# A three-mixer transformer and a mixture of experts in one program: two token row groups of the input projection moved into the mixers

## What is computed

```python
for l in range(DEPTH):                    # DEPTH = 2
    h = x @ w_cols                        # 3400 columns, 3432 in the second layer
    o_gla  = _gla_mixer(gq, gk, gv, gg, galr, ...)
    o_rwkv = _rwkv7_mixer(rr, rk, rv, rwlr, ralr, rglr, ...)   # token shift first
    o_nsa  = _nsa_mixer(h_nsa, pos, ...)  # rotary q and keys, compressed blocks, gates
    mix = jnp.concatenate([o_gla, o_rwkv, o_nsa], axis=-1) @ w_out[l]
    x = _layer_norm(DEEPNORM_ALPHA * x + mix, ln1_w[l], ln1_b[l])
    ffn = (jax.nn.silu(x @ ffn_w_gate[l]) * (x @ ffn_w_up[l])) @ ffn_w_down[l]
    x = _layer_norm(DEEPNORM_ALPHA * x + ffn, ln2_w[l], ln2_b[l])
```

## Time and profile before

| | |
|---|---|
| median of 3 runs | 2019.58 us (2018.89 to 2026.96) |
| the profiled execution | 2023.03 us, its span 2021.2 us |
| TensorE (PE) busy | 1966.1 us, 97% |
| VectorE (DVE) busy | 855.1 us, 42% |
| ScalarE (ACT) busy | 313.4 us, 16% |
| mean granted TensorE clock | 0.993 |

### The profile page before, as it was taken

One profiled execution on the slowest core, in us unless ns is written; L12 is line 12 of the kernel. 1 busy time (PEld: TensorE's weight loads), 2 busy tenths in 40 slices (PEclk: granted clock), 3 DMA queues, 4 the chain that ended last, 5 costly groups with the idle time before them and its releaser, 6 DMA issues.

```text
span 2021.2 us, 24513 instructions
## 1 busy us (share of the span) xinstructions
PE 1966.1 (97%) x9835; PEld 1115.1 (55%) x9835; DVE 855.1 (42%) x1538; ACT 313.4 (16%) x725; POOL 45.1 (2%) x62
## 2 busy tenths in 40 slices
PE   8999999999999999999999999999999999999997
PEld 7878588748777588749553333333333333333332
DVE  1487588865587586754731111111111111111112
ACT  1335211101435111103410000000000000000001
POOL 0021000000021000000000000000000000000000
PEclk9999999999999999999999999999999999999999
DMA  8540067646630165436298999999999999999996
GB/s 332 217 158 1 32 234 308 251 167 278 263 126 1 41 226 199 171 154 266 89 393 373 428 429 429 427 429 429 427 430 427 430 429 427 429 427 430 429 428 287
DMA packets 44275, 598.75 MB, mean 296 GB/s; under 512 B 5056, under 2 KB 5360, under 8 KB 8464
## 3 DMA queue, kind: packets, MB, share of 16 engines
q1 hardware_dynamic: 44208, 597.82, 71.9%
HBM read 596.73 MB, written 1.07 MB: 296 GB/s over the span
## 4 chain that ended last, share of the span: by engine, by line
PE 82%; DMA 15%; DVE 3%; issue 0%; ACT 0%; SPq 0%; DVEq 0%
PE ps L2349 18%; DMA ring<-in_stream 15%; PE ps L1404 12%; PE ps L2397 8%; PE ps L1489 7%; PE ps L402 6%; PE ps L2323 3%; PE ps L1273 3%; PE ps L361 2%; PE ps L2338 2%; PE ps L419 2%; PE ps L2434 2%; PE ps L1820 1%; PE ps L1986 1%; PE ps L1150 1%; PE ps L1167 1%
## 5 line engine op out<-in xcount | busy, mean ns | idle before, releaser
L2349 PE MATMUL ps<-ring,HT 128*64 128x512 f32 x2176 | 479.4, 594 | 20.0 <-DMA ring<-in_stream 19.2
L2349 PEld LDWEIGHTS ps<-ring,HT 128*64 128x64 f32 x2176 | 152.9, 137 | 340.1 <-issue 289.3
L2397 PE MATMUL ps<-SB,HT 128*64 128x512 f32 x1088 | 249.2, 612 | 0.9 <-ACT HT L2460 0.9
L2505 DVE TENSOR_SCALAR HT<-ps 128x512 f32<-128x512 f32 x34 | 23.5, 692 | 449.8 <-PE ps L2349 449.8
L2397 PEld LDWEIGHTS ps<-SB,HT 128*64 128x64 f32 x1088 | 77.0, 140 | 170.2 <-issue 170.2
L1404 PE MATMUL ps<-ring,SB 128*128 128x256 f32 x704 | 156.0, 379 | 0.3 <-DVE SB L331 0.3
L2454 ACT ACTIVATE HT<-HT 128x512 f32<-128x512 f32 x34 | 21.5, 631 | 843.9 <-DVE HT L2505 843.9
L1404 PEld LDWEIGHTS ps<-ring,SB 128*128 128x128 f32 x704 | 133.6, 190 | 18.8 <-issue 0.7
L2517 DVE TENSOR_TENSOR HT<-ps,TOK 128x512 f32<-128x512 f32 x34 | 23.5, 692 | 281.3 <-PE ps L2397 281.3
L402 PE MATMUL ps<-SB,ring 128*128 128x256 f32 x576 | 126.9, 384 | 1.3 <-DMA ring<-in_stream 1.3
L402 PEld LDWEIGHTS ps<-SB,ring 128*128 128x128 f32 x576 | 110.8, 193 | 17.1 <-issue 1.6
(11 more groups left out here) (489 smaller groups left out, 2251.8 us busy)
## 6 DMA issues: line engine op xcount, KB each, us to landing
ring<-in_stream SPq DMA_DIRECT2D x210, 2048.0 KB, 16.6
SB<-in_stream SPq DMA_DIRECT2D x68, 2048.0 KB, 24.8
SB<-in_ln SPq DMA_DIRECT2D x8, 512.0 KB, 7.0
CST<-in_const SPq DMA_DIRECT2D x1, 1362.0 KB, 5.5
PAR<-in_layer SPq DMA_DIRECT2D x2, 558.5 KB, 11.6
X<-in_x SPq DMA_DIRECT2D x1, 1024.0 KB, 4.9
HN<-in_head_norm SPq DMA_DIRECT2D x2, 512.0 KB, 12.8
SB<-in_cond_row SPq DMA_DIRECT2D x2, 512.0 KB, 10.9
```

The lines of the kernel that those rows point to most:

```text
L2349: m = pe.matmul(ps[HD * half:HD * (half + 1), a, :], XE[:, 2 * b + k, q * SLOTS_E:(q + 1) * SLOTS_E], w[:, k, a, half, :], start=False, st ...
L2397: m = pe.matmul(ps[HD * c:HD * (c + 1), 3, :], EHT[:, k, HD * b:HD * (b + 1)], w[:, k, c, :], start=b + k == 0, stop=b + k == 4, skip_grou ...
```

## The change

The two layers do the same in both kernels. The groups are cut and ordered anew:

- Group 11 is now the 24 gate columns of all tokens (16 products, L408 of the changed kernel). Groups 12 and 13 are the tokens' 512 columns (the former 13 and 14), group 14 the 256 value columns of all tokens (16 products of 256 columns).
- Ahead of the mixers TensorE now does groups 0 to 8, gate, ranks, group 9, two rotations, norm, groups 10 and 11, group 12.
- Group 13 stands in turns 2 to 6 of the mixers, as one, one, two, two and two products, and the unread products of turns 2 to 7 are gone. Group 14 stands in steps 2 and 3 (4, then 6 and 2 in step 2, 4 in step 3), and the 15 unread products there are gone.
- On VectorE the first two rotations move from the mixers into the GLA decay. On ScalarE the copy of group 10 moves behind the query, beside that of group 11. The waits of later readers are set to the new counts; the compressed blocks (`cmp_pool`) lie elsewhere and wait for `rw_ops`.

```diff
-                return "proj_ready", 15 * l + [2, 4, 6, 8, 10, 13, 15][s]
+                return "proj_ready", 15 * l + [2, 4, 6, 8, 10, 15, 14][s]
...
-            return g % 4 if g < 13 else g - 9
+            return g % 4 if g < 12 else (4, 7, 3)[g - 12]
...
+        def project_pe(pe, l, groups):
+            for g in groups:
+                need_slot(pe, AT["in", l, g // 2])
+                w = slot(AT["in", l, g // 2]).rearrange("p (k n) -> p k n", k=KT)
+                if g >= 4:
+                    pe.wait_ge(S("proj_evac"), 15 * l + g - 3)
+                if g == 10:
+                    pe.wait_ge(S("rope"), ROPE_PIECES * l + 2)
...
+        def project_gates_pe(pe, l):
+            w = slot(AT["in", l, 5]).rearrange("p (k n) -> p k n", k=KT)
+            pe.wait_ge(S("proj_evac"), 15 * l + 8)
+            pe.wait_ge(S("rope"), ROPE_PIECES * l + 2)
+            for t in range(NT):
+                for k in range(KT):
+                    m = pe.matmul(ps[:, proj_bank(11), 24 * t:24 * (t + 1)], XT[:, k, t * P:(t + 1) * P], w[:, k, 384:408],
+                                  start=k == 0, stop=k == KT - 1)
+            m.then_inc(S("proj_ready"), 1)
...
+        def project_tokens_pe(pe, l, t, ks):
...
+            for k in ks:
+                m = pe.matmul(ps[:, proj_bank(12 + t), :], XT[:, k, t * P:(t + 1) * P], w[:, k, 0:512],
+                              start=k == 0, stop=k == KT - 1)
...
+        def project_values_pe(pe, l, t, ks):
...
+                m = pe.matmul(ps[:, proj_bank(14), t * 256:(t + 1) * 256], XT[:, k, t * P:(t + 1) * P], w[:, k, P:P + 256],
+                              start=k == 0, stop=k == KT - 1)
...
             ins.then_inc(S("gla_zb"), 1)
+            rope_dve(v, l, 0, I, L)
+            rope_dve(v, l, 1, I, L)
             v.wait_ge(S("gla_zb"), l + 1)
             v.wait_ge(S("gla_lp"), l + 1)
...
+        TOKEN_PIECES = (range(0, 1), range(1, 2), range(2, 4), range(4, 6), range(6, 8))
...
-                else:
-                    pe.wait_ge(S("rope"), ROPE_PIECES * l + 3)
-                    clock_pe(pe, 7, 0, 256, 1)
+                elif u < 7:
+                    project_tokens_pe(pe, l, 1, TOKEN_PIECES[u - 2])
...
                 if s == GLA_BACK:
-                    clock_pe(pe, 3, 0, 256, 3)
+                    project_values_pe(pe, l, 0, range(4))
...
+                if s == GLA_BACK + 1:
+                    project_values_pe(pe, l, 1, range(4, 8))
...
                 if s == GLA_BACK:
-                    clock_pe(pe, 3, 0, 256, 3)
+                    project_values_pe(pe, l, 0, range(4, 8))
+                    project_values_pe(pe, l, 1, range(2))
                     back_pe(pe, 2 * l, G_XC, 4)
-                    clock_pe(pe, 3, 0, 256, 3)
+                    project_values_pe(pe, l, 1, range(2, 4))
...
-                        clock_pe(pe, 3, 0, 256, 6)
+                        pe.wait_ge(S("proj_evac"), 15 * (l + 1))
...
-                    project_pe(pe, l, range(5))
+                    project_pe(pe, l, range(9))
...
                 gla_gate_pe(pe, l)
                 rwkv_ranks_pe(pe, l)
-                project_pe(pe, l, (5,))
+                project_pe(pe, l, (9,))
+                for p in range(2):
+                    rope_pe(pe, l, p)
                 rwkv_norm_pe(pe, l)
-                project_pe(pe, l, (6,))
+                project_pe(pe, l, (10,))
+                project_gates_pe(pe, l)
+                project_tokens_pe(pe, l, 0, range(KT))
...
                 rwkv_gates_act(act, l, I)
-                project_act(act, l, (10,))
                 gla_query_act(act, l)
-                project_act(act, l, (11, 12))
+                project_act(act, l, (10, 11))
                 rwkv_decay_act(act, l, I)
                 rwkv_values_act(act, l)
-                project_act(act, l, (13,))
+                project_act(act, l, (12,))
```

More of the change, by code:

```diff
@@ L383, in project_first_pe @@
                     m.then_inc(S("proj_ready"), 1)
-        def project_pe(pe, l, slots):
-            def bank_free(g):
-                if g >= 13:
+        def project_pe(pe, l, groups):
[6 more added lines that the diff above has]
+                    pe.wait_ge(S("rope"), ROPE_PIECES * l + 2)
+                for j in range(2 if g < 10 else 1):
+                    for k in range(KT):
+                        m = pe.matmul(ps[:, proj_bank(g), j * T:(j + 1) * T],
+                                      w[:, k, (2 * (g % 2) + j) * P:(2 * (g % 2) + j + 1) * P],
+                                      XT[:, k, :], start=k == 0, stop=k == KT - 1)
+                m.then_inc(S("proj_ready"), 1)
@@ L389, in bank_free @@
+        def project_tokens_pe(pe, l, t, ks):
+            w = slot(AT["in", l, 6]).rearrange("p (k n) -> p k n", k=KT)
+            if ks[0] == 0:
+                need_slot(pe, AT["in", l, 6])
+                if t == 0:
                     pe.wait_ge(S("gla_zb"), l + 1)
                     pe.wait_ge(S("rw_gates"), l + 1)
[L391 to L421, removed]
@@ new lines, in project_tokens_pe @@
+                else:
+                    pe.wait_ge(S("rope"), ROPE_PIECES * l + 3)
+            for k in ks:
+                m = pe.matmul(ps[:, proj_bank(12 + t), :], XT[:, k, t * P:(t + 1) * P], w[:, k, 0:512],
+                              start=k == 0, stop=k == KT - 1)
+            if ks[-1] == KT - 1:
+                m.then_inc(S("proj_ready"), 1)
+        def project_values_pe(pe, l, t, ks):
+            w = slot(AT["in", l, 5]).rearrange("p (k n) -> p k n", k=KT)
+            for k in ks:
+                m = pe.matmul(ps[:, proj_bank(14), t * 256:(t + 1) * 256], XT[:, k, t * P:(t + 1) * P], w[:, k, P:P + 256],
+                              start=k == 0, stop=k == KT - 1)
+            if t == NT - 1 and ks[-1] == KT - 1:
+                m.then_inc(S("proj_ready"), 1)
@@ L430, in project_act @@
                     to, n = HT[:, 20, :], T
-                elif g < 13:
-                    to, n = NV[:, g - 11, :], 280
-                else:
-                    to, n = TOK[:, g - 13, :], 512
-                nc.scalar.activation(to, ps[:, proj_bank(g), 0:n], ACT.Copy,
+                elif g == 11:
+                    to, n = NV[:, :, 256:280], 48
+                elif g < 14:
+                    to, n = TOK[:, g - 12, :], 512
+                else:
+                    to, n = NV[:, :, 0:256], 512
+                come = ps[:, proj_bank(g), 0:n]
+                if g in (11, 14):
+                    come = come.rearrange("p (t c) -> p t c", t=NT)
+                nc.scalar.activation(to, come, ACT.Copy,
                                      scale=HD ** -0.5 if g == 0 else 1.0).then_inc(S("proj_evac"), 1)
@@ L973, in rwkv_norm_dve @@
             nc.vector.tensor_tensor(R_XC, R_XC, GT.rearrange("p t c -> p (t c)"), ALU.mult).then_inc(S("head_out"), 1)
-        flat_xt = XT[:].rearrange("p k t -> p (k t)")
-        N_FL = [view(flat_xt, 1024 + 512 * i, [16, 32]) for i in range(2)]
+        N_FL = [view(SB, 10240 + 512 * i, [16, 32]) for i in range(2)]
         N_GE = [view(SB, at, [256]) for at in (10240, 10496, 11264)]
@@ L2647, in mixers_act @@
                     head_norm_act(act, 2 * l)
+                if u == 1:
+                    project_act(act, l, (14,))
                 if unit_scores(u):
@@ L2742, in _ @@
                         project_first_pe(pe, l, t)
[L2743 removed]
+                    project_pe(pe, l, range(2, 9))
                 gla_gate_pe(pe, l)
                 rwkv_ranks_pe(pe, l)
[L2746 removed]
+                project_pe(pe, l, (9,))
+                for p in range(2):
+                    rope_pe(pe, l, p)
                 rwkv_norm_pe(pe, l)
[L2748 removed]
+                project_pe(pe, l, (10,))
+                project_gates_pe(pe, l)
+                project_tokens_pe(pe, l, 0, range(KT))
                 rwkv_bonus_pe(pe, l)
```

20 lines of the change are left out of this document (8 added, 12 removed).

## The result

The changed kernel takes 2066.06 us (median of 4 runs, 2063.66 to 2067.59), the kernel before beside it 2019.24 (4 runs). The ratio is 1.0223, with a 95% interval of 1.0195 to 1.0251: slower, by 46.8 us in the medians. The profiled span is 2064.3 us against 2021.2, 43.1 more, and the mean granted clock 0.98 against 0.993.

The account below looks back on a forecast made before the run. TensorE was taken to bound the kernel; L738 delays 3.6 + 7.7, mixers 8.6 + 3.0 and clock 4.2 + 1.6 gave 28.7 us on the profiled 2023.0, so 2051.7, or 2048 on the median's scale; range 2037 to 2058.

Parts of the forecast that it names:

- the order's mechanism: Ahead of the mixers: group 9's copy delays ScalarE's decay 5.2 and 7.6 us, so TensorE idles at norm 6.8 and 7.5.
- The waits and products: Both layers at full clock, without any clock fall: 22.9 us added, giving 2042.5.
- The stretch ahead of the mixers: Projection up to L738: waits outweigh 10.9 us less work per layer, so L738 starts 3.6 and 7.7 us later.
- The narrow products: Group 11's sixteen 24-column gate products on TensorE, set by their weights: 3.7 us.
- The waits' sizes: TensorE idle, layer 0: 2.0 at ranks, 6.8 norm, 2.1 transposes, 3.2 before L738; layer 1: 3.5, 7.5, 4.2 at the first three.
- The rotations on VectorE: Six passes, 4.1 us, fit into the wait for the decay and cost nothing; without that wait they cost 4.1.
- The mixers: Tokens' and value products replacing unread ones add 4.3 us a layer in the turns and 1.5 in step 2.
- The clock: TensorE's idles drop the granted clock to half: 4.2 us for long waits plus 1.6 for short ones, 5.8 together.
- one sure fall: Behind the 6.8 and 7.5 us waits for the gates, half clock costs 2.1 us in each layer, 4.2 together.
- one of three: Of three 3.1 to 3.5 us idles (before L738 in both layers, layer 1's ranks), one falls: 1.6, bounds 0 to 4.8.
- The rival of more falls and slow returns: All three short idles count and tokens 0 also run at half clock: 39.5 us added, some 2059; chance 0.07.
- The rival on the other side: Earlier gate product carries through if copies of groups 9 and 11 do not hold decay and root: 2014.2; chance 0.06.

Follow-up runs that it names:

- ScalarE's order: Changed kernel with only ScalarE reordered: decay, gates and query ahead of group 9's copy, root ahead of the copies of groups 10 and 11; 2048.39 us, ratio 1.0153.
- the mixers' half alone: Changed kernel's groups and mixers, with ranks behind group 9, norm and rotations behind the gate columns, VectorE's rotations back in the mixers; 2039.88 us, ratio 1.0089.
- the version with all waits filled: Changed kernel plus unread products in TensorE's four waits per layer (ahead of ranks, norm, transposes, mixers), nothing else; 2044.97 us, ratio 1.0119.

## Why the prediction was wrong

The direction and the order's mechanism were right, the price of the clock was not: 2048 with a range to 2058, measured 2066.06. Of the 18 us between, 15.3 are the clock's. Another 3.7 are the scale: the profiled execution of the kernel before lay 3.8 above its median, so that 43.1 more in the profiles are 46.8 in the medians; what it lost there isn't shown. The waits and products came out 0.9 smaller.

- *The stretch ahead of the mixers*, right. Steps gave +3.6 and +7.7 for L738; filled with work, so that the clock stays, it came within 0.1 us of the step in layer 0. The narrow products took 3.65, as reckoned (3.7). The waits' sizes were right to 0.2 us except the transposes' (0.86 and 2.58 against 2.1 and 4.2): at half clock norm took 2.05 instead of 1.10 and so 1 us of each, and 0.3 and 0.6 were sized wrong.
- *The rotations on VectorE*, right for this order: they end before the decay's functions do. Wrong was their price without that cover, 4.1: there they wait for their product behind group 9 first.
- *The mixers*, nearly right: +4.1 in the turns at full clock (4.3), +1.3 and +1.4 behind them (1.5); 5.4 for the whole half, measured apart, against 5.8.
- *The clock*, the step that failed. The "one sure fall" behind each wait for the gates was put at 2.1 a layer, and cost about that. What was mis-sized is the term for the short idles, "one of three" at 1.6, with none for layer 0's 1.96 us. All four were followed by half clock, and they cost 16.9: 4.9 and 5.6 at the ranks, 3.2 in the turns of each layer. The earlier trace rows gave the level of the clock, but not how long it stays there. After the ranks' wait of layer 0 half clock lasted ten busy microseconds, through the ranks and most of group 9, and not for one group's 1.6. In all, the clock cost 21.1 against 5.8.
- *The rival of more falls and slow returns* (0.07) was the nearest, with 2059. It let the clock come back late behind the long waits, where tokens 0 in fact ran at full clock (7.11), and had no fall behind layer 0's ranks.
- *The rival on the other side* named the copies of groups 9 and 11 as what holds the chain. With them out of the way alone (ScalarE's order) the kernel is still 29 us behind. The rotations had to come ahead of group 9, and the keys and the gate columns to be mended, before anything was gained. Its 2014.2 is then about what was reached, 2014.7 and 2012.97.

The Trainium skill (TensorE: Matmul & The Clock Gate, "Why this matters for your kernels") warns of idle gaps between bursts of matmuls. The traces agree (0.50 behind the 6.91 us idle), and show more here: idles as short as 1.4 to 2.0 us were followed by half clock in some stretches and not in others. At the ranks the profiled executions can be counted. With a wait of 1.96 or 3.39 ahead of them the clock fell in five of six stretches; with no idle over 0.2 us it fell in three of eighteen, in or right behind the ranks of layer 1 each time. So the waits aren't the only way to a fall, and what decides stays open.

## What to carry to other kernels

Before moving a small product ahead of a large group, list on every engine what stands in its queue between the small product's operands and the group: here a copy on ScalarE and the rotations on VectorE both held the chain until the group was done. Price an idle of TensorE by itself plus the work behind it that would run at half clock, several microseconds even for an idle of two (4.9 here), and put real work into it or, where there is none, unread products. When a mended wait gives no time, look for the next one before giving the mend up: here two edits gave next to nothing apart, and 4 to 6 us together.

## What the hardware showed that was not expected

Sixteen 24-column products in one stretch came with a fall of the clock to half, without an idle of TensorE, in seven of the fourteen such stretches profiled (two a kernel). The longest idle in the ten microseconds ahead of such a fall is 0.65. Six of the other seven stretches came right behind a return of the clock, but so did one of the seven with a fall (the mixers' half alone, layer 1), so the return doesn't settle it. Woven between 512-column products, the same sixteen left it at 1.00 in all six stretches.

A fall also came far from any long wait, at the mixers' late steps, in the profiled execution of the version with all waits filled (windows of layer 0):

```profile
220.00:235.00 15.00, 15.00 (x77) 11.18 (x76) 3.56 (x16) 3.09 (x12) 0.00 (x0) 0.50 0.00 1
```

TensorE is busy for all of these 15 us at half clock. That execution took 2056.1, the other four of the version 2040.34 to 2046.02, so the fall is hardly in every execution. Why it came there isn't settled.
